# Experts picked four at a time, routing and expert loop in one block, and weight requests issued during the output projection

## The reference

```python
x = x + mixer(rmsnorm(x))                      # RWKV7 and gated-delta heads, ends in @ w_out
x = x + memory_cross_attention(rmsnorm(x))     # ends in @ wo
x = x + routed_ffn(rmsnorm(x))                 # below
y = rmsnorm(x)

def routed_ffn(h):                             # 288 tokens, 32 experts, 4 of them for each token
    logits = h @ router_w + router_b
    top_v, top_i = lax.top_k(logits, 4)
    gates = softmax(top_v)
    for each expert e, for the tokens that chose it:
        hc  = h_e @ w1[e] + b1[e]              # 1024 -> 2048
        hg  = min(hc[:, :1024], 7)
        hl  = clip(hc[:, 1024:], -7, 7)
        act = hg * sigmoid(1.702 * hg) * (hl + 1)
        y_e = act @ w2[e] + b2[e]              # 1024 -> 1024
        out[tokens] += gate * y_e
```

## Time and profile before

| | |
|---|---|
| median of 3 runs | 1596.72 us (1596.07 to 1601.69) |
| profiled execution | 1599.83 us |
| its span | 1598.1 us |
| PE, DVE, ACT, POOL busy | 94%, 32%, 15%, 4% of the span |
| HBM read | 463.40 MB, of it 403 MB experts' weights |
| 700 to 1500 us | PE busy all the time, DMA share 1.00, 430 GB/s |
| 600 to 650 us (routing) | PE busy 32.94 us of 50, 342 GB/s |

### The profile page before, as it was taken

The page is one execution under the profiler, slowest core; times in us unless marked ns, Lnnn a source line. Parts: engine busy times, 40 slices in busy tenths (PEclk is TensorE's granted clock), DMA queues, the critical chain, the costliest instruction groups (busy, mean ns, idle before and its releaser), DMA issues.

```text
span 1598.1 us, 23835 instructions
## 1 busy us (share of the span) xinstructions
PE 1497.6 (94%) x9767; PEld 732.9 (46%) x9767; DVE 514.6 (32%) x1075; ACT 235.2 (15%) x531; POOL 59.9 (4%) x103
## 2 busy tenths in 40 slices
PE   5999978798799997799999999999999999999997
PEld 4776666797647745233333333333333333333332
DVE  2484514523510503322323224223232232232333
ACT  2334201231002403000001001000000010000002
POOL 3010100230000000000000000000000000000000
PEclk9999989898798996899999999999999999999999
DMA  5332254100525727699999999999999999999972
GB/s 159 103 106 86 78 146 118 30 4 13 183 110 234 290 106 329 270 421 430 431 425 433 429 433 430 425 432 431 427 434 429 428 435 427 430 430 428 435 299 110
DMA packets 74649, 471.28 MB, mean 295 GB/s; under 512 B 14660, under 2 KB 48155, under 8 KB 58080
## 3 DMA queue, kind: packets, MB, share of 16 engines
q1 hardware_dynamic: 73804, 469.68, 71.9%
q10 hardware_dynamic: 788, 0.78, 0.2%
HBM read 463.40 MB, written 7.05 MB: 294 GB/s over the span
## 4 chain that ended last, share of the span: by engine, by line
PE 59%; DMA 0%; DVE 0%; ACT 0%; SPq 0%; issue 0%
PE ps L2791 28%; PE ps L2822 14%; PE ps L2411 6%; PE ps L2770 4%; PE ps L2783 2%; PE ps L2418 1%; PE ps L2764 1%; PE ps L2808 1%; PE ps L2813 1%; DMA b<-in_b_e_dram 0%; DVE eh_tm L2915 0%; PE ps L2835 0%; ACT eh_tm L2862 0%; SPq L2728 0%; ACT y L2853 0%
## 5 line engine op out<-in xcount | busy, mean ns | idle before, releaser
L2822 PE MATMUL ps<-w,big 128*64 128x512 f32 x1024 | 226.8, 595 | 0.0
L2881 DVE TENSOR_SCALAR big<-ps 128x512 f32<-128x512 f32 x32 | 22.1, 692 | 606.0 <-PE ps L2791 606.0
L2822 PEld LDWEIGHTS ps<-w,big 128*64 128x64 f32 x1024 | 70.7, 137 | 133.3 <-issue 133.3
L500 PE MATMUL ps<-yT,wst 128*128 128x288 f32 (+1 forms) x496 | 126.8, 415 | 0.0
L2791 PE MATMUL ps<-wa,big 128*64 128x512 f32 x512 | 116.1, 607 | 0.0
L2791 PE MATMUL ps<-wc,big 128*64 128x512 f32 x512 | 113.4, 595 | 0.0
L2791 PE MATMUL ps<-wd,big 128*64 128x512 f32 x512 | 112.6, 592 | 0.0
L2791 PE MATMUL ps<-wb,big 128*64 128x512 f32 x512 | 112.6, 592 | 0.0
L500 PEld LDWEIGHTS ps<-yT,wst 128*128 128x128 f32 (+1 forms) x496 | 93.5, 191 | 30.5 <-issue 5.2
L2411 PE MATMUL ps<-eh_tm,sel 128*64 128x512 f32 (+1 forms) x396 | 98.6, 616 | 1.3 <-DVE sel L2438 1.3
L2873 DVE TENSOR_TENSOR x<-x,ps 128x1024 f32<-128x1024 f32 x66 | 80.2, 1216 | 45.7 <-PE ps L2770 45.7
(11 more groups left out here) (622 smaller groups left out, 1576.0 us busy)
## 6 DMA issues: line engine op xcount, KB each, us to landing
w<-in_w_e_dram SPq DMA_DIRECT2D x64, 2048.0 KB, 15.0
wb<-in_w_e_dram SPq DMA_DIRECT2D x16, 4096.0 KB, 19.6
wa<-in_w_e_dram SPq DMA_DIRECT2D x16, 4096.0 KB, 16.6
wc<-in_w_e_dram SPq DMA_DIRECT2D x16, 4096.0 KB, 17.5
wd<-in_w_e_dram SPq DMA_DIRECT2D x16, 4096.0 KB, 20.6
wst<-in_w_in_dram SPq DMA_DIRECT2D x15, 1024.0 KB, 5.5
kvc<-in_cache_mem_k_dram SPq DMA_DIRECT2D x5, 1024.0 KB, 9.3
kvc<-in_cache_mem_v_dram SPq DMA_DIRECT2D x5, 1024.0 KB, 7.2
```

The costliest lines, as they stand in the source:

```text
L500: ins = nc.tensor.matmul(ps[:q.n, 6 + t % 2, 0:T], wst[:, q.group % NG, c, q.at:q.at + q.n], hT[:, c, :], start=(c == 0), stop=(c == KC - 1))
L2822: ins = nc.tensor.matmul(ps[CAP * half:CAP * half + CAP, 2, :], actT[:, c, h, :], w2[:, h, c, 512 * half:512 * half + 512], start=(h == 0 ...
L2881: nc.vector.tensor_scalar(hg[:, :], ps[:, 0, :], LIMIT, None, ALU.min).then_inc(hg_ok, 1)
```

## The change

Four things change together, all from the attention's output projection on.

1. *Requests in the output projection.* SyncE issues there the router's weights, the second half of W1 of item 0, all of W2 of item 0 and all of W1 of item 1. What is left for the routing is b2, b1 and the first half of W1 of item 0, whose buffer the projection itself uses.
2. *Transfers and buffers in two parts.* Each half of W1 comes as two transfers of 2 MB, each half of W2 as two of 1 MB, with a semaphore for each and a release for each (`w1_used`, `w2_used`).
3. *One block.* Routing and loop are one block: eight items follow the routing directly, then comes a loop with eight items in its body (one round here), then 16 more items written out. The last four gather nothing.
4. *Picking by four.* `gather(c, b)` runs once in each item and takes a quarter of the rows (chunk c of each half) for the next four items at once. The output is already turned, so `turn_x` and ScalarE's copy go; VectorE's `take_x` writes it out times the norm's weights. The matrices `sel` are made once in four items, with 4 x 64 columns.

```diff
+    def first_experts(self, sp):                       # SyncE, in the output projection
+        sp.dma_start(self.rw, a["router_w"]...); sp.dma_start(self.gfx, ...); sp.dma_start(self.rb, ...)
+        for g in range(2):
+            load_w1(sp, a, self, 1, g)
+        for q, (h, g) in enumerate(PART):
+            sp.dma_start(part_of(self.w2[:, h], g), w2_part(self.w2_d, h, g, slice(0, 1))).then_inc(self.w2_in[q], 16)
+        for q, (h, g) in enumerate(PART):
+            sp.dma_start(part_of((self.wc, self.wd)[h], g), w1_part(self.w1_d, h, g, slice(1, 2))).then_inc(
+                self.w1_in1[q], 16)
...
-        def gather():
-            for i, (t0, n) in enumerate(TILES):
-                for half in range(2):
-                    ins = nc.tensor.matmul(ps[CAP * half:CAP * half + CAP, 3, :], sel[:n, i, :],
-                                           h_tm[:n, i, 512 * half:512 * half + 512], start=(i == 0),
-                                           stop=(i == 2))
+        def gather(c, b):
+            for h in range(2):
+                for i in range(2):
+                    nc.tensor.matmul(ps[:, b + h, 0:4 * CAP], h_tm[:, i, P * (HK * h + c):P * (HK * h + c) + P],
+                                     sel[:, i].rearrange("p e t -> p (e t)"), start=(i == 0), stop=False)
+            for j in range(4):
+                r, m = slice(NS * j, NS * j + NS), CAP * (j % 2)
+                ins = nc.tensor.matmul(ps[m:m + CAP, b + j // 2, 0:4 * CAP], hs[r, c, :],
+                                       sel[r, 2].rearrange("p e t -> p (e t)"), start=False, stop=True,
+                                       tile_position=(NS * j, m))
             ins.then_inc(gath_done, 1)
...
+        def take_x(dst, c, b):
+            nc.vector.tensor_tensor(dst, ps[:, b:b + 2, 0:4 * CAP].rearrange("p h (e t) -> p h e t", e=4),
+                                    over(over(gfx[:, :, c], 4, 2), CAP, 3), ALU.mult).then_inc(xT_ok, 1)
...
+                    def next_w1(k, s):                 # SyncE
+                        e = expert(k + 2)
+                        for q, (h, g) in enumerate(PART):
+                            sp.wait_ge(w1_used, 4 * k + q + 1)
+                            sp.dma_start(part_of(w1[s % 2][h], g), w1_part(w1_d, h, g, e)).then_inc(w1_in[s % 2][q], 16)
+                            if q == 0:
+                                load_b1(sp, e, s % 2)
+                    def next_w2(k):
+                        e = expert(k + 1)
+                        for q, (h, g) in enumerate(PART):
+                            sp.wait_ge(w2_used, 4 * k + q + 1)
+                            sp.dma_start(part_of(w2[:, h], g), w2_part(w2_d, h, g, e)).then_inc(w2_in[q], 16)
...
+                    def item(j, o, s, more_x):         # TensorE
+                        if s % 4 == 0:
+                            pe.wait_ge(xT_ok, k + 4)
...
+                        for h in range(2):
+                            for c in range(HK):
+                                if c % 2 == 0:
+                                    pe.wait_ge(w1_in[s % 2][2 * h + c // 2], 64 * j + 16 * p + 16)
...
+                                if c % 2:
+                                    ins.then_inc(w1_used, 1)
...
+                        combine(0, 6)
+                        if more_x:
+                            pe.wait_ge(sel_ok, 2 * j + 2 * o + s // 4 + 2)
+                            pe.wait_ge(xT_ok, k + 4)
+                            gather(s % 4, 3)
+                            pe.wait_ge(add_ok, 3 * k + 1)
+                        combine(1, 6 if more_x else 3)
...
-                    gather()
+                    for c in range(2):                 # TensorE, routing: the first four items
+                        gather(c, first_bank[c])
...
+                    for c in range(2, 4):
+                        pe.wait_ge(xT_ok, c - 1)
+                        gather(c, first_bank[c])
...
+                    for s in range(8):
+                        item(0, 0, s, True)
+                    pe.wait_ge(tab_ok, 1)
+                    more = extra_rounds(pe)
+                    with pe.Fori(0, more) as j:
+                        for s in range(8):
+                            item(j, 1, s, True)
+                    for s in range(8):
+                        item(more, 1, s, True)
+                    for s in range(8):
+                        item(more, 2, s, s < 4)
```

More of the change, by code:

```diff
@@ L158, in build @@
         ahead = Ahead(nc, a, outer, sb)
[L159 to L163, removed]
+        kvb = sb(outer, "kvb", [P, KC * NM + NB * 260])
+        mixer(nc, a, out, ahead, sb, ps, ident, ones, x, g8, stat, eps, norm_stage, kvb)
+        ahead.big = kvb
+        attention(nc, a, out, ahead, sb, ps, ident, ones, x, g8, stat, eps, *kv_views(kvb))
+        experts(nc, a, out, ahead, sb, ps, ident, ones, x, g8, stat, eps)
 class Tiles:
@@ L2340 @@
 HK = 4
+PART = [(h, g) for h in range(2) for g in range(2)]
 NQ = P
@@ L2491, in _ @@
                         sp.dma_start(y[sides[half], :], a["b2_e"][0][:, 512 * half:512 * half + 512]).then_inc(b2_in, 16)
[L2492 to L2496 removed]
+                    for s in range(2):
+                        load_b1(sp, slice(s, s + 1), s)
@@ new lines, in _ @@
+                    with sp.Fori(0, more) as j:
+                        for s in range(8):
+                            next_w1(8 * j + 8 + s, s)
+                            next_w2(8 * j + 8 + s)
+                    for s in range(15):
+                        if s < 14:
+                            next_w1(8 * more + 8 + s, s)
+                        next_w2(8 * more + 8 + s)
+                    sp.wait_ge(w1_used, 32 * more + 96)
+                    sp.dma_start(gf, a["final_norm"].partition_broadcast(P)).then_inc(gf_in, 16)
@@ L2628, in _ @@
+                    for half in range(2):
+                        r = slice(CAP * half, CAP * half + CAP)
+                        nc.vector.tensor_copy(pick[r, :, :], over(ident[r, CAP * half:CAP * half + 2], CAP, 2))
                     nc.vector.tensor_copy(rep4, over(ident[:NS, :NS], 4)).then_inc(rep_ok, 1)
@@ new lines, in _ @@
+                    for s in range(8):
+                        item(0, 0, s, True)
+                    dve.wait_ge(tab_ok, 1)
+                    more = extra_rounds(dve)
+                    with dve.Fori(0, more) as j:
+                        for s in range(8):
+                            item(j, 1, s, True)
+                    for s in range(8):
+                        item(more, 1, s, True)
+                    for s in range(8):
+                        item(more, 2, s, s < 4)
+                    for at, i in enumerate(ends):
+                        dve.wait_ge(cmb_done, 24 * more + 73 + at)
+                        add(i, last_bank[i], xs_ok if i == 2 else added)
```

716 lines of the change are left out of this document (352 added, 364 removed).

## The result

The changed kernel takes 1591.57 us in the median of 20 runs, beside 1597.05 for the kernel before on the same chip: a ratio of 0.9967 [0.9956, 0.9978]. The forecast was 1565.5 with a range of 1554 to 1586. The sign was right, but a sixth of the gain came, and the time lies outside the range.

A forecast was written before the change was run, and what follows sets the result against it. It took DMA as the bound after the change: 650.8 + 2.4 + 30.33 x 29.64 = 1552.2, plus 1.8 and 12.9 gave a span of 1566.9, 31.2 less. So 1596.7 - 31.2 = 1565.5 us, range 1554 to 1586.

The forecast's parts named there:

- Start of item 0: At the end of routing: TensorE starts item 0 at about 646.2 us, 3.7 us earlier than before.
- TensorE's item: In the loop: without `turn_x` (-0.59) and with a gather of 2.36 us, an item takes 28.0 us.
- last four: The last four items gather nothing, so each takes TensorE 28.0 - 2.4 = 25.6 us.
- DMA's pace: In the loop: DMA needs 29.64 us an item, 29.39 plus 0.25 for more packets.
- the waits begin at item 13: In the loop: from about item 13 on TensorE waits 1.6 us an item for W2, not for W1.
- TensorE then has the last quarter of W2 to do, 1.8: 1554.0: At the loop's end: after DMA's end at 1552.2 only 1.8 us of TensorE's work remain, ending at 1554.0.
- A: In the loop: TensorE stays the bound with a gather of 3.7 us and items of 29.35: 1582; chance 0.12.
- B: Before item 0: low clock through all gathers, a start 8 us later: 1574, or 1577 with slow item 0; chance 0.10.
- C: In the written-out loop: TensorE waits 1.8 us for each of 37 packets of instructions: 1611; chance 0.05.
- D: In the loop: the clock falls in waits for W2, costing 3.7 us an item: 1663; chance 0.02.
- E: In the loop: nothing gained, as with DMA slower by 1 us an item from eight requests: 1596; chance 0.04.

The follow-up runs named there:

- same_w2: The changed kernel with W2 loaded for item 0 only, later requests for W2 bringing 256 bytes: 1561.92 us.
- whole: The changed kernel with the experts' weight transfers and their releases in one part again (4 MB for half of W1, 2 MB for half of W2): 1585.32 us.
- w2_first: The changed kernel with W2 of the next item asked for between W1's halves for items 20 to 23, ahead of all W1 from item 24: 1578.42 us.
- no_gather: The changed kernel with the items' gather shrunk from eight matmuls to one small one: 1586.62 us.
- before_b1: The kernel before, with the requests for b1 of items 0 and 1 put first in the routing: 1596.02 us.
- ends_in_parts: The changed kernel with whole transfers and W2 asked for ahead in the last items, but W1 of items 2, 30 and 31 in parts: 1574.26 us.
- by_rows: The changed kernel with whole transfers, each issued as two, for partitions 0 to 63 and 64 to 127: 2510.22 us.

## Why the prediction failed

Counted from the projection's start it was 27.5 us short. Point by point:

1. *Start of item 0*: forecast 75.25, measured 75.41. The first gather began 1.5 us earlier against the projection than forecast, the four gathers took 1.7 longer (15.3 from the first to item 0). Clock up at item 0, as said. Right.
2. *TensorE's item*: gather 2.36 forecast, 2.51 measured; item 28.0 and 28.27; last four 25.6 and 27.55. Together the path was 17.6 us too short (`same_w2`). The two terms, 28 x 0.27 = 7.6 and 4 x 1.95 = 7.8, are most of it; the rest lies in item 0 (28.79) and in the low clock of item 28 (29.15). It reached the end only through item 31 (point 5), since DMA was the later of the two. The second term is an error of method: I took the gather's time out of the last items without asking what it covered.
3. *DMA's pace*: 29.64 us an item forecast, 29.90 measured. From the first request (80.12 after, 79.85 forecast) and 2.4 us, 30 items' worth pass until the last quarter of W2 of item 30, landed at 1548.1, is used at about 1548.7, which is 979.4: (979.4 - 80.12 - 2.4) / 30. The base that I read from the growing queue in the earlier trace rows, 29.39, is 29.47 in `whole`; the packets of the parts add 0.41 in the mean (0.34 in undisturbed items), where my line from the earlier trace rows gave 0.35 and I took 0.25. By that item 30 has its W2 8.1 us late. The mechanism was right, the term too small. That the waits begin at item 13, as I had said, is partly luck: I had 20 us of lead and a loss of 1.6 an item, and it lost 1.3 an item (29.59 less 28.27), which makes 17 in 13 items.
4. **The step that failed: "TensorE then has the last quarter of W2 to do, 1.8: 1554.0".** From the last landing (1558.6) to the copy (1579.84) 21.2 us pass. I treated DMA's queue and TensorE's path as two sums of which the later holds, and joined them at the last byte. But W2 has one buffer, and SyncE asks for W1 of item k+2 ahead of W2 of item k+1. So 8 MB for item 31 come ahead of W2 of item 30, and the transfer that TensorE waits for last is W2 of item 30. Behind it lies all of item 31. The order of requests was in the description of the kernel, and that W2 would be waited for and not W1 was in my own prediction. With my own numbers the sum is the last byte less one W2 (29.64 / 3), 1542.3, and the last quarter, 1.8, and an item without gather, 25.6: 1569.7 instead of 1554.0, and a time of 1581. That is 15.7 us. `w2_first` shows it by turning the order over: 14.6 us come back, with neither a byte nor a matmul changed. That this is so near to 15.7 is partly luck, since other waits and the low clock stand in its last items.
5. *Item 31 itself* takes 29.3 us (1550.58 to 1579.84) and not 25.6: 3.7. Of these 1.95 are the activation that the gather used to cover, the others nearly all the clock, which is down in it: at full clock it takes 27.7 (`same_w2`, `no_gather`).

15.7 + 8.1 + 3.7 are the 27.5. Of the rivals, A had DMA's side wrong (TensorE waits from item 13 on, as forecast), B did not come. C fell: 77 packets of instructions, where I expected 80, and no pause on TensorE that they would explain; items 1 to 12 follow each other without any:

```profile
q8 instruction: 77, 1.26, 0.3%
```

The Trainium skill (Runtime: NRT & Kernel Launch, Instruction fetch mechanics) has it that fetches in sequence are mostly hidden; this trace agrees. D fell in the loop: with waits of 0.55 us the granted clock stays at 1.00 up to 1500 us. In the last items, with pauses of 1.93 us, 1560 to 1580 has 0.91, and W2 of item 31 takes 8.13 for 7.09. The pause alone doesn't explain it, since items 29 to 31 of `same_w2` have it at full clock; what does is open. E gave the number that came closest, but by another mechanism: its DMA item was to be 1 us longer, the measured one is 0.5 above 29.39.

What each part of the change is worth, by the profiles: the start 3.6 (2.1 of it, the earlier first logits, by the router's early request; that b1 and the block border pay for the four gathers is reasoned, not run), the 12 MB of other early requests 0. With whole transfers 7.3 more come (`whole` ends 10.9 before the kernel of before, less 3.6 for the start). They belong to picking by four and to the clock in item 0 (28.79 us for 32.72) together, and no run takes these apart. The parts cost 7.2 and take just that back. With the order mended more is left of it: `before_b1`, with the old gather and items of 29.11, ends at 1023.50, and `ends_in_parts` at 1002.72. That the old gather would hold the latter up is argued from the two, not run.

## What to carry to other kernels

- Where a queue of transfers becomes the bound, don't end the sum at its last byte. Write down the order of the requests, find the transfer that is waited for last, and add all the work that depends on it. In the last rounds, ask first for what is used first, even if the steady state likes another order.
- A faster engine beside a queue that is already full gives what the queue has left: here the item of 29.11 us stood beside a queue of 29.39, and the gain had to come from the ends.
- Before an instruction's time is taken off a path, ask what it covers: without the gather of 2.5 us an item is only 0.7 us shorter, as TensorE then waits for the other engines.
- Splitting a transfer along the free axis buys an early release and costs its packets. Split where a release stands on the critical path, not everywhere.

## What the runs showed of the hardware

- Transfers for 64 neighbouring partitions (0 to 63, then 64 to 127) run at half the rate (211 GB/s), and the share of busy DMA engines doesn't tell: it reads 1.01 there and in the changed kernel with 424 GB/s. Two transfers for the even and the odd partitions run at the full rate (431 GB/s). The Trainium skill (DMA: Bandwidth & Descriptors, The descriptor swizzle) says that partitions 0 to 63 and 64 to 127 are reached by different ports; by that, such a transfer has half of the ports. The runs agree.
- A packet costs some 11 ns beside its bytes (10 to 13 by the three ways of counting above), over sizes of 32, 16, 8 and 4 KB.
- In `by_rows`, where TensorE waits 23.5 and 3.6 us for weights in an item, the mean granted clock was 0.77; with waits of 0.55 us in the changed kernel it stayed at 1.00 up to 1500 us. With pauses of 1.93 us it fell in some items (28 of `same_w2`, 29 to 31 of the changed kernel) and not in others (29 to 31 of `same_w2`).
